# Triangular inverses by 32x32 blocks in column groups, in a two-layer hybrid decoder kernel

## What is computed

```python
decay = where(tril, exp(G_i - G_j), 0)
L = where(strict, (kb @ k.T) * decay, 0)          # strictly lower triangular
T = triangular_solve(eye + L, eye, lower, unit_diagonal)
u = T @ vb
w = T @ (kb * exp(G))
```

## Time and profile before

| | us |
|---|---|
| median of 3 runs | 2061.95 (2061.73 to 2062.51) |
| the profiled execution | 2061.8 |
| its span | 2060.0 |
| PE busy | 1980.1 (96%) |
| DVE busy | 1122.2 (54%) |
| ACT busy | 779.4 (38%) |
| POOL busy | 426.8 (21%) |
| mean granted clock of PE | 0.988 |

### The profile page before, as it was taken

The page is one execution under the profiler, slowest core; times in us unless marked ns, Lnnn a source line. Parts: engine busy times, 40 slices in busy tenths (PEclk is TensorE's granted clock), DMA queues, the critical chain, the costliest instruction groups (busy, mean ns, idle before and its releaser), DMA issues.

```text
span 2060.0 us, 25541 instructions
## 1 busy us (share of the span) xinstructions
PE 1980.1 (96%) x9988; PEld 1595.8 (77%) x9988; DVE 1122.2 (54%) x1702; ACT 779.4 (38%) x1182; POOL 426.8 (21%) x240
## 2 busy tenths in 40 slices
PE   7899999999989999999999999999999999999999
PEld 5678988667777888888876889876777778888887
DVE  7955558553385555543369265576433855555422
ACT  5542253653253323222254422536433533322221
POOL 3446012232161000000045350122411700000000
PEclk9999999999999999999999989999999999999999
DMA  5331012212162333333342210122121622233333
GB/s 202 115 121 60 10 61 82 82 56 83 56 233 89 96 103 92 98 102 102 113 163 98 80 64 17 62 87 72 67 72 62 235 92 93 92 98 97 103 102 102
DMA packets 60973, 196.45 MB, mean 95 GB/s; under 512 B 10560, under 2 KB 11072, under 8 KB 58688
## 3 DMA queue, kind: packets, MB, share of 16 engines
q1 hardware_dynamic: 44832, 152.49, 23.5%
q10 hardware_dynamic: 16032, 42.41, 5.4%
HBM read 176.01 MB, written 18.87 MB: 95 GB/s over the span
## 4 chain that ended last, share of the span: by engine, by line
PE 82%; DVE 10%; ACT 2%; POOL 2%; DMA 2%; issue 1%; POOLq 0%; SPq 0%; ACTq 0%; DVEq 0%; PEldq 0%
PE bank L489 21%; PE bank L491 21%; PE bank L490 21%; PE bank L744 2%; PE bank L724 2%; PE bank L937 2%; PE bank L864 2%; PE bank L981 1%; PE bank L734 1%; DVE arena L1995 1%; DMA raw<-weights 1%; PE bank L873 1%; DVE wL L1455 1%; POOL wL L2067 1%; PE bank L845 1%
## 5 line engine op out<-in xcount | busy, mean ns | idle before, releaser
L489 PE MATMUL bank<-hH,wH 128*128 128x512 f32 (+1 forms) x1536 | 616.6, 401 | 22.9 <-DVE hL L1464 9.7
L491 PE MATMUL bank<-hH,wL 128*128 128x512 f32 (+1 forms) x1536 | 605.1, 394 | 0.0
L490 PE MATMUL bank<-hL,wH 128*128 128x512 f32 (+1 forms) x1536 | 604.6, 394 | 0.0
L2067 POOL TENSOR_TENSOR wL<-raw,wH 128x1024 fp32r<-128x1024 f32 (+1 forms) x114 | 278.7, 2449 | 1146.6 <-ACT wH L1085 1146.5
L1085 ACT ACTIVATE wH<-raw 128x1024 fp32r<-128x1024 f32 (+1 forms) x276 | 287.9, 1045 | 257.5 <-PE bank L491 216.3
L489 PEld LDWEIGHTS bank<-hH,wH 128*128 128x128 f32 (+1 forms) x1536 | 290.9, 189 | 101.0 <-issue 26.6
L491 PEld LDWEIGHTS bank<-hH,wL 128*128 128x128 f32 (+1 forms) x1536 | 290.2, 189 | 64.2 <-issue 0.6
L490 PEld LDWEIGHTS bank<-hL,wH 128*128 128x128 f32 (+1 forms) x1536 | 290.8, 189 | 61.0 <-issue 1.8
L1455 DVE TENSOR_TENSOR wL<-raw,wH 128x1024 fp32r<-128x1024 f32 x162 | 214.1, 1322 | 211.6 <-ACT wH L1085 210.9
L489 PE MATMUL bank<-hidH,wH 128*128 128x512 f32 x352 | 139.8, 397 | 0.0
L491 PE MATMUL bank<-hidH,wL 128*128 128x512 f32 x352 | 138.6, 394 | 0.0
(11 more groups left out here) (398 smaller groups left out, 2760.9 us busy)
## 6 DMA issues: line engine op xcount, KB each, us to landing
raw<-weights SPq DMA_DIRECT2D x279, 512.0 KB, 3.5
gates<-gst ACTq DMA_DIRECT2D x64, 256.0 KB, 2.4
gload<-gates ACTq DMA_DIRECT2D x16, 1024.0 KB, 7.3
arena<-weights ACTq DMA_DIRECT2D x10, 512.0 KB, 5.4
xT<-x SPq DMA_DIRECT2D x4, 512.0 KB, 5.8
pj<-weights ACTq DMA_DIRECT2D x4, 512.0 KB, 4.1
out<-xT SPq DMA_DIRECT2D x8, 256.0 KB, 4.4
const<-constants SPq DMA_DIRECT2D x1, 1100.5 KB, 7.1
```

Of the source, the lines that this page charges most:

```text
L489: mm(out, a[0], b[0], start=start, stop=False)
L490: mm(out, a[0], b[1], start=False, stop=False)
L491: return mm(out, a[1], b[0], start=False, stop=stop)
L2067: tt_(l, x, h.bitcast(F32), SU).then_inc(slab_taken[i % RING], 1)
```

## The change

All 16 matrices are now inverted in two stages. First the four 32x32 diagonal blocks of each matrix are inverted by doubling (levels 1 to 4), kept as narrow tiles of 128 rows (4 blocks) x 32 columns: `ua` is U, `utb` its transpose, `lc32` the diagonal blocks of L, `lm32` those blocks masked for each level (POOL), `mU` the full 128x128 block-diagonal form of U. A product has a 32-wide stationary tile and a 128-wide moving operand, and four matrices in succession write the four column groups (32 partitions each) of one bank. Transposes are products with the identity. Then two joining levels: the fifth joins pairs of 32 into 64, with `lo32`, the blocks next to the diagonal; the last joins the two 64 halves with products of 64x64. The matrices go in two halves of 8. Diagonal blocks are copied out of and into the full matrices in pieces of 32 partitions, two on DVE and two on ACT. The starting transposes, 64 products of 32x32, stand ahead of the two filler tiles `skq`. The filler tile of the levels is run in eighths, two behind each of levels 1 to 4; ACT evacuates it after all levels. POOL clears `mU` and `mT`, and masks `lc32`, ahead of its next weight splits.

```diff
-        "turn": 0, "skq": 2, "level": [0, 0, 0, 0, 1, 0], ...
+        "turn": 0, "skq": 2, "level": [1], ...
...
+        ybd = mats[2]
+        ua, utb, lo32, lc32 = (arena[:, 6144 + 512 * i:6656 + 512 * i].rearrange("p (u c) -> p u c", u=16) for i in range(4))
+        def rows(b):
+            return slice(32 * b, 32 * b + 32)
+        def of_half(x, g):
+            return x[:, 8 * g:8 * g + 8]
+        def cols32(b, at=slice(0, P)):
+            return PS[b][at, 0:256].rearrange("p (u c) -> p u c", u=8)
...
 PE
+                    pe.wait_ge(*of("bt_taken", 6))
+                    for g in range(2):
+                        for u in range(8 * g, 8 * g + 8):
+                            for b in range(4):
+                                last = mm(PS[(2, 7)[g]][rows(b), 32 * (u % 8):32 * (u % 8) + 32], mL[rows(b), u, rows(b)],
+                                          cst("id32")[rows(b), :], start=True, stop=True)
+                        last.then_inc(q["y_ps"], 1)
                     fill(FILL["skq"])
-                    (16 transposes, y_product, t_transpose, u_product, six levels)
+                    pe.wait_ge(*of("at_part", 4))
+                    def at4(u):
+                        return rows(u % 4), slice(P * (u // 4 % 2), P * (u // 4 % 2) + P)
+                    for n in range(1, 6):
+                        pe.wait_ge(*(of("low_masked", n) if n < 5 else of("low_blocks", 2)))
+                        for g in range(2):
+                            k = 2 * (n - 1) + g
+                            pe.wait_ge(*of("u_ready", 2 * k + 1))
+                            for u in range(8 * g, 8 * g + 8):
+                                at, c = at4(u)
+                                last = mm(PS[3 + g][at, c], ua[:, u, :], ident, start=True, stop=True)
+                            last.then_inc(q["t_ps"], 1)
+                            pe.wait_ge(*of("u_ready", 2 * k + 2))
+                            pe.wait_ge(*of("u_copied", k + 1))
+                            for u in range(8 * g, 8 * g + 8):
+                                at, c = at4(u)
+                                last = mm(PS[(2, 7)[g]][at, c], lm32[n - 1][:, u, :], mU[:, u, :], start=True, stop=True)
+                            last.then_inc(q["y_ps"], 1)
+                        for g in range(2):
+                            pe.wait_ge(*of("t_ready", k + 1)); pe.wait_ge(*of("y_ready", k + 1)); pe.wait_ge(*of("y_copied", k + 1))
+                            for x in range(2 * g, 2 * g + 2):
+                                for b in range(4) if n < 5 else (0, 2):
+                                    last = mm(PS[5 + g][rows(b), P * (x % 2):P * (x % 2) + P], utb[:, 4 * x + b, :],
+                                              ybd[:, 4 * x + b + n // 5, :], start=True, stop=True)
+                            last.then_inc(q["du_ps"], 1)
+                        if n < 5:
+                            part(2)
+                    (then per half: 8 transposes and 8 products of 64x64, and after copies 8 products of 64x64)
...
 ACT
-                    for n in range(24):
-                        a.wait_ge(*of("t_ps", n + 1))
-                        act(mT_flat[...], PS[6 + n % 2][:, :], ACT.Copy).then_inc(q["t_ready"], 1)
+                    a.wait_ge(*of("at_part", 4))
+                    for b in range(4):
+                        last = act(lc32[rows(b), :, :], mL[rows(b), :, rows(b)], ACT.Copy)
+                    last.then_inc(q["low_blocks"], 1)
+                    def diagonal(k):
+                        a.wait_ge(*of("u_ready", 2 * k + 1))
+                        for b in (2, 3):
+                            last = act(of_half(mU[rows(b), :, rows(b)], k % 2), of_half(ua[rows(b)], k % 2), ACT.Copy)
+                        last.then_inc(q["u_copied"], 1)
+                    a.wait_ge(*of("u_zeroed", 3))
+                    (diagonal(0), diagonal(1), two copies into lo32)
+                    for n in range(1, 6):
+                        for g in range(2):
+                            a.wait_ge(*of("t_ps", k + 1))
+                            act(of_half(utb, g), cols32(3 + g), ACT.Copy).then_inc(q["t_ready"], 1)
+                            a.wait_ge(*of("y_ps", k + 3))
+                            for c in (2, 3):
+                                last = act(of_half(ybd[rows(c), :, rows(c)], g), cols32((2, 7)[g], rows(c)), ACT.Copy)
+                            last.then_inc(q["y_copied"], 1)
+                        (diagonal of each half; for n = 5 a copy of the joined block)
+                    (copies of the 64-wide step)
+                    fill(FILL["level"][0])
...
 DVE
+                    (per half: mask the transposed blocks, ua = I - masked, diagonal copies of rows 0 and 1)
+                    for n in range(1, 6):
+                        for g in range(2):
+                            v.wait_ge(*of("y_ps", k + 3))
+                            for c in (0, 1):
+                                last = nc.vector.tensor_copy(of_half(ybd[rows(c), :, rows(c)], g), cols32((2, 7)[g], rows(c)))
+                            last.then_inc(q["y_ready"], 1)
+                        for g in range(2):
+                            v.wait_ge(*of("du_ps", 2 * (n - 1) + g + 1))
+                            if n < 5:
+                                tt_(of_half(ua, g), of_half(ua, g), cols32(5 + g), SU).then_inc(q["u_ready"], 1)
+                                diagonal(2 * n + g)
...
 POOL
                     g.wait_ge(*of("qd_ready", 8))
+                    g.wait_ge(*of("bt_ps", 6))
+                    g.memset(mU_flat[:, :], 0.0).then_inc(q["u_zeroed"], 1)
+                    g.memset(mT_flat[:, :], 0.0).then_inc(q["u_zeroed"], 1)
+                    g.wait_ge(*of("at_part", 4))
+                    g.memset(lo32, 0.0).then_inc(q["u_zeroed"], 1)
+                    g.wait_ge(*of("low_blocks", 1))
+                    for n in range(1, 5):
+                        tt_(lm32[n - 1], lc32, lev[:, n, :].unsqueeze(1).broadcast_to([P, 16, 32]), M).then_inc(q["low_masked"], 1)
                     low_of(BEFORE_NSA + 2)
```

More of the change, by code:

```diff
@@ new lines, in _ @@
+                    for g in range(2):
+                        pe.wait_ge(*of("u_ready", 21 + g))
+                        pe.wait_ge(*of("u_copied", 11 + g))
+                        for u in range(8 * g, 8 * g + 8):
+                            c = slice(HD * (u % 8), HD * (u % 8) + HD)
+                            last = nc.tensor.transpose(PS[3 + g][0:64, c], mU[0:64, u, 0:64], ident[0:64, 0:64])
+                        last.then_inc(q["t_ps"], 1)
+                        for u in range(8 * g, 8 * g + 8):
+                            c = slice(HD * (u % 8), HD * (u % 8) + HD)
+                            last = mm(PS[(2, 7)[g]][0:64, c], mL[64:128, u, 0:64], mU[64:128, u, 64:128], start=True, stop=True)
+                        last.then_inc(q["y_ps"], 1)
@@ L745, in u_product @@
+                    for g in range(2):
+                        pe.wait_ge(*of("y_ready", 11 + g))
+                        pe.wait_ge(*of(("y_copied", "t_ready")[g], 11))
+                        for u in range(8 * g, 8 * g + 8):
+                            last = mm(PS[5 + g][0:64, HD * (u % 8):HD * (u % 8) + HD], ut64[:, u, :], y64[:, u, :],
                                       start=True, stop=True)
                         last.then_inc(q["du_ps"], 1)
-                    pe.wait_ge(*of("kc_ready", 1))
@@ L1764, in _, with eight @@
[L1764 to L1772 removed]
+                    def eight(x):
+                        return x.unsqueeze(1).broadcast_to([P, 8, 32])
@@ new lines, in diagonal @@
+                    def diagonal(k):
+                        v.wait_ge(*of("u_ready", 2 * k + 1))
+                        for b in (0, 1):
+                            last = nc.vector.tensor_copy(of_half(mU[rows(b), :, rows(b)], k % 2), of_half(ua[rows(b)], k % 2))
+                        last.then_inc(q["u_ready"], 1)
+                    v.wait_ge(*of("at_part", 4))
+                    for g in range(2):
+                        v.wait_ge(*of("y_ps", g + 1))
+                        step(tt_(of_half(utb, g), cols32((2, 7)[g]), eight(lev[:, 0, :]), M))
+                        tt_(of_half(ua, g), eight(cst("id32")), of_half(utb, g), SU).then_inc(q["u_ready"], 1)
+                        if g == 0:
+                            v.wait_ge(*of("u_zeroed", 2))
+                        diagonal(g)
```

175 lines of the change are left out of this document (74 added, 101 removed).

## The result

The changed kernel took 2016.03 us, median of 4 runs (2012.19 to 2019.53), beside 2062.16 us for the kernel before on the same chip (2061.73 to 2062.51): ratio 0.9776 with a 95% interval of 0.9758 to 0.9794. Five more runs in a later comparison gave 2015.58 (2014.75 to 2016.33), before 2062.99, ratio 0.9773. The forecast was 2014.5, in a range of 2001 to 2038.

What follows compares the result with a forecast made beforehand. PE bounds the kernel: busy 96% of the span, 82% of the chain. Per layer 25.5 us won less 1.8 of clock is 23.75, 47.5 for two: 2061.8 to 2014.3, on the median 2014.5; range 2001 to 2038.

Steps and rivals of the forecast that it cites:

- the stretch: Per layer, from the work behind the K K' products to the first W product: 25.5 us to be won.
- Small products: 64 starting products of 32x32 ahead of the fill tiles: 128 records in 3.6 us, ends 1.8 and 7.
- Lead-in through ACT and POOL: Ahead of level 1: PE idles 5.3 us behind ACT's evacuation, split and copies, then POOL's mask.
- Narrow records: Products with 32-wide stationary tiles in four column groups, in the levels: 0.0287 us per record.
- The rival with the full pitch: In the levels, column groups do not overlap: 0.111 us per record, 12.1 us per level, 2075 us; chance 0.04.
- the crossing: Level period from which the full-pitch rival decides between faster and slower: about 10.5 us.
- A level: Each doubling level: 4.13 us of PE work, period 4.9 us with PE waiting 0.75 for ACT.
- that rival: In the levels, ACT is the bound: 32-partition copies cost 0.66 us, period 6.3, total 2029.7; chance 0.15.
- Half clock: After PE's pause ahead of level 1: 1.2 GHz for about 3.7 us, level 1 2.0 us longer.
- DVE against POOL: DVE's diagonal copies of level 1 beside POOL's work: 0.5 us lost, ends 0 and 2.4.
- Clock behind the last steps: Half clock once more after the 64-column step: 1.8 us lost in the work behind.
- fifth level and last steps: Fifth level starts at 230.8, its u-products end at 234.3; after the 64-column step, W product at 240.05.

Runs made afterwards that it cites:

- The experiment with early masks: Changed kernel with ACT's compact and diagonal copies ahead of its last evacuation and weight split, lower blocks at level 2: 2013.35 us, ratio 0.9773.
- the one-group run: Changed kernel with all transposing and y-products writing column group 0, not the true inverses: 2063.93 us in one run.
- The divided part: Changed kernel with three fill matmuls behind each half's u-products instead of six behind both: 2012.77 us, ratio 0.9769.
- The late splits: Changed kernel with POOL's two weight splits waiting until DVE has finished level 4: 2014.44 us, ratio 0.9774.
- the run with both the busy pause and the late splits: Changed kernel with 24 unread matmuls added in PE's pause ahead of level 1 and POOL's splits behind level 4: 2010.32 us, ratio 0.9755.
- the last version: Changed kernel with early masks, splits behind level 4, divided fill parts, and lower blocks copied by POOL: 2002.53 us, ratio 0.9707.

## Why the prediction was right, point by point

The time came out 1.5 us above the forecast. Per layer 25.5 us were to be won in the stretch and 1.8 given back behind it, 23.75 in all; the stretch won 23.7 and 24.0, and nothing was seen to be given back right behind it. This is closer than the terms deserve: several are off and cancel, and the changed kernel's own runs lie between 2012.19 and 2019.53. That it came within 1.5 us is luck.

- **Small products: too dear.** 1.42 and 1.93 us for 3.6, close to the lower end of 1.8 or under it (1.31 at full clock, 1.93 at half). Level 1 starts 19.6 us into the stretch instead of 21.5, 1.9 sooner than forecast, for this reason. The pitch of the 32-column tile, 0.0287, was the wrong row for them.
- **Lead-in through ACT and POOL: right.** PE idle for 5.66 us (5.3 forecast), released by POOL's mask at L2191, ACT's copies at 0.63 each where 0.49 was taken. The experiment with early masks shows the queue position to be the cause, since the pause follows it.
- **Narrow records: right.** 0.029 us. The rival with the full pitch fell, and the one-group run, with the u-products still spread, shows what it would have been: at a period of 10.3 us the kernel takes 2063.93, the time before, where the prediction had put the crossing at about 10.5. The Trainium skill (TensorE: Matmul & The Clock Gate, Part 1) gives some 62 ns for a matmul that is decoded by microcode. No row tells how these were decoded, and counted per product of two records the narrow ones take 58 ns, which decides nothing; but the 64 small products take 1.36 us, 21 ns each, so that figure did not bind here.
- **A level: 5.41 us instead of 4.87.** The mechanism was right (PE waits 0.51 us for ACT's 32-partition copies; they cost 0.38 each and not 0.66, so that rival fell); three terms were short. From the first transposing product at 222.01 the second u-products start at 3.25 (forecast 3.05), since ACT's two pieces take 0.76 and not 0.67; from there to the fill 0.58 (0.46); the fill 1.59 (1.37). The last two are the changes between narrow products and fill matmuls, which the sum had at nothing: 0.34 per level. The divided part shows it again with 0.33, and the kernel before shows that 0.11 of it comes without narrow tiles.
- **Half clock: right as to its coming and its depth, wrong as to its length and its cost.** The clock was at 0.50 for 6.8 us from 206.2, 5.3 of them behind the start of level 1, where the prediction had 3.7 us from 208.7. It had 2.0 us for it in level 1; the runs with and without the added matmuls, splits late in both, differ by 0.7 and 0.9 in that level. So a dip that was longer than forecast cost less than half. The remainder of level 1's extra was ACT, arriving at its first evacuation behind its own lead-in copies; the total, 7.10 for 7.4, hid this.
- **DVE against POOL: the upper end, not 0.5.** Level 2 was 7.2 us, 2.3 over the forecast, of which 1.8 over a plain level. The late splits show that to be POOL's. The Trainium skill (SBUF — State Buffer, Who interferes with whom) has this as an exclusive port pair that a copy from SBUF to SBUF can take, and that one side holds for its whole instruction. The trace agrees: each of the two copies ended 0.14 or 0.15 us behind the POOL instruction that was in flight when it started. The prediction's range stopped at one instruction, 2.4 us, but a half's diagonal copies are two, and each meets a split of its own: 2.7 us here, 3.6 in the early-mask run.
- **Clock behind the last steps: not there.** 1.8 us were set down; the stretch 245 to 250 ran at 1.00. But this was chance. In the second profile of the same kernel the dip did come, in layer 0's PE timeline and stretch:

```profile
243.07 3.22 PE L791 MATMUL bank<-arena,pj 128*64 128x128 f32 x32 [0.87 <-DVE arena L1838]
```

```profile
243.60:247.00 3.40, 2.93 (x28) 2.53 (x24) 0.00 (x0) 1.54 (x4) 2.06 (x1) 0.50 0.16 37
```

The first fill matmul behind the W product came 8.18 us after it, not 6.81: 1.4 us of the 1.8. It also came in the run with both the busy pause and the late splits (0.75 from 240 to 245). So the term was right for some executions, and hangs on small shifts.

Summed against the forecast for layer 0: 1.9 less for the lead-in and 0.3 less for level 1, then 2.3, 1.0 (two levels) and 0.7 (fifth level and last steps) more make 1.8 more, and the 1.8 of clock not lost takes it back. The terms that were mis-sized are those between neighbours: POOL's splits beside DVE, set at 0.5 us and measured at 1.9 (layer 0, by the late splits), the edges of the fill part, set at nothing and measured at 0.34 a level, and the half clock, set at 2.0 and measured at 0.7 to 0.9. The small products, set at 3.6 and measured at 1.4 to 1.9, were the largest miss the other way.

## What to carry to other kernels

A faster engine exposes the order of the queues that feed it: of the 20.2 us that the last version wins in the two stretches beyond the change, dividing the fill on PE alone gives 2.4, 1.25 lie in fill tiles that met less half clock, and the rest came with copies and a wait moved on ACT's and POOL's queues. Before counting a narrow tile's pitch, check that its neighbours go to other column groups, and count the changes between narrow products and wide ones as items of their own. Keep long POOL instructions away from short DVE copies on the loop's path, count such a wait once for each copy, and take away a clock loss and a wait for POOL together, for one alone hides the other. Before comparing a stretch between kernels, see where the half clock fell in each: here it moved the same fill tiles by 1.5 us.

## What the runs showed of the hardware that was not expected

- Two DVE copies that take 0.58 us together took 3.25, 4.21 and 4.39 us when they met two POOL instructions of 2.4 us back to back. The first copy was let in between them and the second was not let in before their end: each ended 0.14 or 0.15 us behind one POOL instruction.
- Changing from 128x32 stationary tiles to 128x128 fill matmuls and back costs 0.33 to 0.34 us, wherever the fill stands; 0.11 of it is there with full tiles on both sides too.
- Column groups help in both orders of the products tried within 16 records; all in one group costs 0.111 us per record instead of 0.029.
- 32x32 products with 32 moving columns take 0.010 us a record at a granted clock of 1.00 and 0.015 at 0.50 (128 in 1.31 and 1.93 us), with one row group as with four. Why they are so short is open.
- The granted clock fell at other places in two profiles of the same kernel, with the same work (0.50 from 243.6 to 247.0 us in one, 1.00 in the other).
- ACT takes as long for 32 partitions as for 128: 0.38 us for 256 columns from PSUM, at L1298 with 128 partitions and in each of L1301's two with 32. From SBUF to SBUF a piece of 32 partitions and 256 columns takes 0.42 us (L1285, four in 1.70). So the 0.66 us in row group 8 is not the price of 32 partitions; the stride is what else is different there, which was not tried.
